# Turning the gathered rows while they are gathered, and a shorter routing stage, in a one-core hybrid layer with a mixture of experts

## What is computed

```
logits = x2 @ router_w + router_b                     # 32 experts
top_vals, top_idx = lax.top_k(logits, TOP_K)          # TOP_K = 4
gates = jax.nn.softmax(top_vals, axis=-1)
...
gu = xb @ w_gu[e] + b_gu[e]                           # rows of expert e, 1024 -> 2048
gate = jnp.minimum(gu[:, :D_FF], SWIGLU_LIMIT)
up = jnp.clip(gu[:, D_FF:], -SWIGLU_LIMIT, SWIGLU_LIMIT)
h = (up + 1.0) * (gate * jax.nn.sigmoid(SWIGLU_ALPHA * gate))
return h @ w_down[e] + b_down[e]                      # 1024 -> 1024
...
y = segment_sum(y_rows * row_w[:, None], row_tok)     # back to the tokens, weighted
```

## Time and profile before

| | |
|---|---|
| time, median of 3 runs | 1216.87 us (1216.04 to 1221.18) |
| the profiled execution's own time | 1217.71 us |
| its span, first to last instruction | 1215.9 us |
| TensorE busy | 1156.7 us, 95% |
| VectorE busy | 513.6 us, 42% |
| ScalarE busy | 254.9 us, 21% |
| bytes moved by DMA | 443.69 MB, mean 365 GB/s; 427 to 428 GB/s through the experts |
| first half and routing | 0 to 289.9 us |
| experts | 289.9 to 1198 us |
| last layer norm and output | 1198 to 1215.9 us |

### The profile page before, as it was taken

One profiled execution on the slowest core, in us unless ns is written; L12 is line 12 of the kernel. 1 busy time (PEld: TensorE's weight loads), 2 busy tenths in 40 slices (PEclk: granted clock), 3 DMA queues, 4 the chain that ended last, 5 costly groups with the idle time before them and its releaser, 6 DMA issues.

```text
span 1215.9 us, 14046 instructions
## 1 busy us (share of the span) xinstructions
PE 1156.7 (95%) x5736; PEld 562.1 (46%) x5736; DVE 513.6 (42%) x977; ACT 254.9 (21%) x398; POOL 3.2 (0%) x12
## 2 busy tenths in 40 slices
PE   9999999999999999999999998999999999999994
PEld 8989999654333333333333323333333333333331
DVE  4888878663333232223332222323222222222236
ACT  4645565311111111111111111111111111111112
POOL 1000000000000000000000000000000000000000
PEclk9999999999999999999999999999999999999998
DMA  9756754646999999999999999999999999999993
GB/s 234 237 168 206 230 146 143 263 179 258 408 430 428 425 429 428 428 426 426 430 427 425 429 427 427 429 427 426 428 428 427 427 428 428 426 427 429 427 424 154
DMA packets 93399, 443.69 MB, mean 365 GB/s; under 512 B 7848, under 2 KB 65336, under 8 KB 67998
## 3 DMA queue, kind: packets, MB, share of 16 engines
q1 hardware_dynamic: 93246, 442.67, 89.8%
q10 hardware_dynamic: 96, 0.22, 0.0%
HBM read 441.34 MB, written 1.53 MB: 364 GB/s over the span
## 4 chain that ended last, share of the span: by engine, by line
PE 57%; DMA 29%; DVE 10%; issue 2%; ACT 2%; DVEq 0%; SPq 0%; ACTq 0%
DMA ring<-in_w_gu 24%; PE PS L821 20%; PE PS L854 13%; PE PS L734 6%; PE PS L649 5%; DMA ring<-in_w_down 3%; PE PS L756 3%; PE PS L667 2%; DVE w_lo L960 2%; DVE tiles L998 2%; DVE tiles L1062 1%; PE PS L742 1%; PE PS L790 1%; PE PS L749 1%; PE PS L894 1%
## 5 line engine op out<-in xcount | busy, mean ns | idle before, releaser
L821 PE MATMUL PS<-ring,mid 128*64 128x512 f32 x1920 | 424.6, 596 | 24.5 <-DMA ring<-in_w_gu 24.5
L821 PEld LDWEIGHTS PS<-ring,mid 128*64 128x64 f32 x1920 | 135.6, 137 | 307.4 <-issue 256.2
L854 PE MATMUL PS<-ring,mid 128*64 128x512 f32 x960 | 212.6, 595 | 0.0
L1261 DVE TENSOR_SCALAR PS<-PS 128x512 f32<-128x512 f32 x30 | 21.0, 700 | 368.5 <-PE PS L821 368.5
L649 PE MATMUL PS<-x_hi,w_hi 128*128 128x320 f32 x448 | 142.4, 318 | 3.9 <-DVE w_lo L960 3.9
L649 PE MATMUL PS<-x_hi,w_lo 128*128 128x320 f32 x448 | 139.7, 312 | 0.0
L649 PE MATMUL PS<-x_lo,w_hi 128*128 128x320 f32 x448 | 139.7, 312 | 0.0
L1243 DVE TENSOR_TENSOR ys<-PS,ys 64x512 fp32r<-64x512 f32 x64 | 44.1, 689 | 200.7 <-ACT ys L567 190.8
L854 PEld LDWEIGHTS PS<-ring,mid 128*64 128x64 f32 x960 | 66.3, 137 | 130.8 <-issue 130.8
L998 DVE SCALAR_TENSOR_TENSOR x_tok<-PS,gate,x_tok 128x1024 f32<-128x1024 f32 (+1 forms) x93 | 115.1, 1276 | 19.7 <-PE PS L756 19.7
L558 ACT ACTIVATE mid<-PS 128x512 f32<-128x512 f32 x30 | 17.9, 597 | 434.2 <-DVE PS L1261 434.2
(11 more groups left out here) (225 smaller groups left out, 731.1 us busy)
## 6 DMA issues: line engine op xcount, KB each, us to landing
ring<-in_w_gu SPq DMA_DIRECT2D x124, 2048.0 KB, 40.0
ring<-in_w_down SPq DMA_DIRECT2D x62, 2048.0 KB, 38.9
raw<-in_w_in SPq DMA_DIRECT2D x56, 512.0 KB, 5.1
ring<-in_w_gu SPq DMA_DIRECT2D x8, 1024.0 KB, 7.4
ring<-in_w_out SPq DMA_DIRECT2D x4, 1024.0 KB, 6.1
ring<-in_w_down SPq DMA_DIRECT2D x4, 1024.0 KB, 41.6
x_tok<-in_x_prompt SPq DMA_DIRECT2D x1, 1024.0 KB, 6.2
out<-x SPq DMA_DIRECT2D x2, 512.0 KB, 2.7
```

What stands on the lines that cost most here:

```text
L821: last = mm(PS[64 * a:64 * a + 64, b, :], xgT[:, 2 * (u % 2) + j, u // 2, :], w[:, o:o + HALF], start=False, stop=(u == 3 and j == 1))
L854: last = mm(PS[64 * a:64 * a + 64, XB, :], hT[:, j, u, :], w[:, j * D + a * HALF:j * D + (a + 1) * HALF], start=(u == 0 and j == 0), stop= ...
L1261: dve.tensor_scalar(gm, gm, LIMIT, None, ALU.min).then_inc(gm_ok, 1)
```

## The change

Five things are done together.

1. `gather` now takes 128 columns of `x1` (every second one) as weights and lets the 64 columns of the one-hot table move, so that the gathered rows come out transposed. It has 8 blocks of 3 multiplications (the three tiles), 24 in all. `turn_x`, one of the two copies and the tile `xg_sb` are gone.
2. In the router the bias is added by TensorE, the logits are taken over tile by tile as they are ready, and the four best of each token are found with `match_replace` and a comparison instead of indices and one-hot sums. The gates come from an exponential over all 32 logits, masked.
3. `mask` and copies of `upper` and `ones` are of type fp32r, and the ranks take 3 multiplications instead of 9 (and 3 more for the counts behind them). `keep_warm` (one fp32r multiplication of 512 columns) replaces `keep_busy` in this stage.
4. The transposes of the position and gate tables (`turn_tables`) move behind the second unit of the first expert, and that expert's `gated_bias` between and into its down units.
5. For the last expert the sums of the one before stand one half unit later (`half == 1`).

The core of the diff:

```
             def gather(count):
                 pe.wait_ge(oh_ok, count)
-                for t, (t0, n) in enumerate(TILES):
-                    for a in range(2):
-                        last = mm(PS[64 * a:64 * a + 64, XB, :], onehot[0:n, t, :],
-                                  x1[0:n, t, a * HALF:(a + 1) * HALF], start=(t == 0), stop=(t == 2))
-                last.then_inc(xg_done, 1)
-
-            def turn_x(src, done):
-
                 for v in range(2):
                     for j in range(2):
-                        last = pe.transpose(PS[:, TB, (2 * v + j) * P:(2 * v + j + 1) * P],
-                                            src[:, 2 * P * v + j:2 * P * (v + 1):2], ident[:, :])
-                last.then_inc(done, 1)
+                        for a in range(2):
+                            first, o = a * HALF + 2 * P * v + j, ((2 * v + j) * 2 + a) * ROWS
+                            for t, (t0, n) in enumerate(TILES):
+                                last = mm(PS[:, XB, o:o + ROWS], x1[0:n, t, first:first + 2 * P - 1:2],
+                                          onehot[0:n, t, :], start=(t == 0), stop=(t == 2))
+                last.then_inc(xg_done, 1)
...
                 if i + 1 < NE:
                     if i + 1 not in ALONE:
                         add_bias(1 - s)
-                    pe.wait_ge(xg_ok, 2 * it + (rows_in(i) + 1))
-                    pe.wait_ge(hT_ok, 2 * it + (i + 1))
-                    turn_x(xg_sb, tx_done)
+                    pe.wait_ge(xgT_ok, 2 * it + (rows_in(i) + 1))
...
+            for q, t in enumerate(T_ORDER):
+                n = TILES[t][1]
+                dve.wait_ge(lg_done, q + 1)
+                link(dve.tensor_copy(lg[0:n, t, 0:NE], PS[0:n, LG_BANK[t], t * NE:(t + 1) * NE]))
+                link(dve.max(top[:, t, :], lg[:, t, 0:NE]))
+                dve.tensor_scalar(ek[:, t, :], lg[:, t, 0:NE], top[:, t, 0:1], None, ALU.subtract).then_inc(top_ok, 1)
+                link(dve.memset(top[:, t, TOPK:], LOWEST))
+                link(dve.match_replace(left[:, t, :], top[:, t, :], lg[:, t, :], HIGHEST))
+                last = dve.tensor_tensor(mask[:, t, :], left[:, t, 0:NE], lg[:, t, 0:NE], ALU.is_gt)
...
+            mm(PS[:, 5, 0:3 * NE], upper_r[:, :], mask[:, :, :].rearrange("p t e -> p (t e)"), start=True, stop=False)
+            mm(PS[:, 5, NE:3 * NE], ones_r[:, :], mask[:, 0:2, :].rearrange("p t e -> p (t e)"),
+               start=False, stop=False)
+            mm(PS[:, 5, 2 * NE:3 * NE], ones_r[:, :], mask[:, 0, :], start=False, stop=True).then_inc(rank_done, 1)
...
-                    if u == 0 and half == 0:
+                    if u == 0 and half == 1:
```

More of the change, by code:

```diff
@@ L197, in hybrid_layer @@
         mid = place("mid", [P, MID_SIZE // 4], MID)
-        xg_sb, xgT_f = (mid[:, i * HALF:(i + 1) * HALF] for i in range(2))
+        th_last, xgT_f = (mid[:, i * HALF:(i + 1) * HALF] for i in range(2))
         ys = place("ys", [P, 2, HALF], MID + 8 * HALF, F32R)
@@ L611, in _, with keep_warm @@
             mm = pe.matmul
+            def keep_warm(n, bank):
+                for _ in range(n):
+                    mm(PS[:, bank, :], ones_r[:, :], bias4[:, 0, :], start=True, stop=True)
             def keep_busy(n, bank):
@@ L697, in logits @@
                 t0, n = TILES[t]
+                out = PS[0:n, LG_BANK[t], t * NE:(t + 2) * NE]
+                mm(out, ones[0:1, 0:n], rb[0:1, :], start=True, stop=False)
+                if q == 2:
+                    keep_warm(3, 1)
                 pe.wait_ge(x1T_ok, q + 1)
                 for k in range(KC):
-                    last = mm(PS[0:n, 4, t * NE:(t + 1) * NE], xT[:, k, t0:t0 + n], rw[:, k, :],
-                              start=(k == 0), stop=(k == KC - 1))
+                    blocks = min(2, KC - k)
+                    last = mm(out[:, 0:blocks * NE], xT[:, k, t0:t0 + n],
+                              rw[:, k:k + blocks, :].rearrange("p a e -> p (a e)"), start=False, stop=(k == KC - 1))
                 return last
             pe.wait_ge(misc_in, 32)
+            pe.wait_ge(pad_ok, 1)
+            pe.wait_ge(consts_r, 1)
+            pe.wait_ge(bias_ok, 1)
             turn_x1(0)
@@ L711, in _ @@
             last.then_inc(so_turned, 1)
-            logits(0)
-            logits(1)
-            keep_busy(3, 1)
+            logits(0).then_inc(lg_done, 1)
+            logits(1).then_inc(lg_done, 1)
+            keep_warm(1, 1)
             turn_x1(2)
-            keep_busy(2, 1)
             logits(2).then_inc(lg_done, 1)
-            keep_busy(12, 1)
+            keep_warm(5, 1)
             pe.wait_ge(mask_ok, 1)
[L721 to L726, removed]
+            mm(PS[:, 5, 0:3 * NE], upper_r[:, :], mask[:, :, :].rearrange("p t e -> p (t e)"), start=True, stop=False)
+            mm(PS[:, 5, NE:3 * NE], ones_r[:, :], mask[:, 0:2, :].rearrange("p t e -> p (t e)"),
+               start=False, stop=False)
+            mm(PS[:, 5, 2 * NE:3 * NE], ones_r[:, :], mask[:, 0, :], start=False, stop=True).then_inc(rank_done, 1)
+            for t in range(3):
+                last = mm(PS[:, 4, 3 * NE:4 * NE], ones_r[:, :], mask[:, t, :], start=(t == 0), stop=(t == 2))
+            last.then_inc(cnt_done, 1)
+            keep_warm(3, 1)
             pe.wait_ge(so_ok, 1)
@@ L961, in split_low @@
                                   ALU.subtract).then_inc(lo_ok, 1)
+            dve.wait_ge(const_ok, 3)
+            dve.tensor_copy(upper_r[:, :], upper[:, :])
+            dve.tensor_copy(ones_r[:, :], ones[:, :]).then_inc(consts_r, 1)
             split_low(0)
@@ L1144, in _ @@
-            link(dve.tensor_copy(small[:, 0:1], ones[:, 0:1]))
-            link(dve.tensor_tensor(lg[0:NS, 2, :], PS[0:NS, 4, 2 * NE:3 * NE], rb[0:NS, :], ALU.add))
-            for t in range(3):
-                last = dve.max(top[:, t, :], lg[:, t, :])
-            link(last)
-            for t in range(3):
-                last = dve.max_index(idx[:, t, :], top[:, t, :], lg[:, t, :])
-            link(last)
-            dve.tensor_copy(idf, idx)
-            dve.tensor_tensor(ek, top[:, :, 0:TOPK], top[:, :, 0:1].to_broadcast([P, 3, TOPK]), ALU.subtract)\
-               .then_inc(top_ok, 1)
@@ L1155, in _ @@
-            dve.wait_ge(top_ok, 1)
-            for t in range(3):
-                last = dve.tensor_tensor(oh4[:, t], iota[:, 0:NE].unsqueeze(1).to_broadcast([P, TOPK, NE]),
-                                         idf[:, t, 0:TOPK].unsqueeze(2).to_broadcast([P, TOPK, NE]), ALU.is_equal)
-            link(last)
-            link(dve.tensor_reduce(mask, oh4.rearrange("p t k e -> p t e k"), AX_X, ALU.add))
-            dve.memset(mask[NS:P, 2, :], 0.0).then_inc(mask_ok, 1)
-            dve.wait_ge(exp_ok, 1)
@@ L1173, in _, with choose @@
+            last.then_inc(mask_ok, 1)
+            def choose(par, e):
+                return dve.tensor_copy(esel4[:, par], where4[:, :, ds(e, 1)].to_broadcast([P, 2, ROWS]))
+            choose(0, 0)
             dve.memset(pos4, 0.0)
+            dve.wait_ge(mask_ok, 1)
             dve.wait_ge(rank_done, 1)
-            dve.tensor_copy(cnt, PS[:, 5, 3 * NE:4 * NE])
-            link(stt(posm[:, :, :], PS[:, 5, 0:3 * NE].rearrange("p (t e) -> p t e", t=3), 1.0, mask, ALU.add, ALU.mult))
-            link(dve.tensor_scalar(posm[:, :, :], posm[:, :, :], -1.0, None, ALU.add))
+            link(stt(posm[:, :, :], PS[:, 5, 0:3 * NE].rearrange("p (t e) -> p t e", t=3), 1.0, mask_f, ALU.add, ALU.mult))
```

163 lines of the change are left out of this document (83 added, 80 removed).

## The result

| | before | after |
|---|---|---|
| time, median | 1216.86 us | 1426.27 us (1424.22 to 1429.02, 4 runs) |
| ratio | | 1.1715, 95% interval 1.1684 to 1.1746 |
| span of the profiled execution | 1215.9 us | 1422.5 us |
| granted clock, mean | 0.992 | 0.902 |
| DMA, mean | 365 GB/s | 312 GB/s |

The change costs 209 us. The forecast was 1390 us with a range up to 1415; the time lies 11 us beyond its top. First the windows of the changed kernel (columns as in the earlier trace rows), then lines of its page: the slices of the granted clock, the chain that ended last, and the group of the new gather.

A forecast was written before the change was run, and what follows sets the result against it. TensorE was to replace DMA as the bound, at 30.9 us an expert. Start 287.5, 30 x 30.95, single places and the end sum to 1309 us; clock falls of +54 to +108 give 1390, range 1246 to 1415.

The forecast's parts named there:

- the threshold: In the experts' stage, any TensorE period above 28.4 us an expert is paid, 30 times.
- the cover: The lead of 10 weight units (49 us of transfers) already there when expert 0 starts, used up over the experts.
- The gather's size: The new gather in each expert takes 8 blocks of 0.92 us, 7.3 us, row changes included.
- The bound of 5.5 for free changes: If row changes cost nothing, the gather takes 5.5 us and the kernel 1251 us; chance 0.14.
- The clock falls in each gather: TensorE drops to 1.2 GHz in each gather: 1363 to 1417 us, taken as 1390; chance 0.50.
- one slow stretch of 1.75 us (1363) and two (1417): Dense work slowed by 1.75 us once for each of 31 gathers, +54 us, or twice, +108 us.
- The reason for the fall: Row changes empty TensorE's array 16 times in the gather's 7.3 us, so the clock level falls.
- The stretch that the prediction held against a fall, 268 to 272 us: Before the experts, only 32-column multiplications and transposes, without row changes or gaps; the clock stayed at 1.00.
- the rival built on that mechanism, 1309 us: The gather never idles, so the clock stays high; TensorE bound at 30.9 us an expert, 1309 us; chance 0.28.
- The routing: Ahead of expert 0, `posm` at 278.3, gather at 279.2 for 284.1, first unit at 287.5, 2.4 us earlier.
- Expert 16: Its gather can't hide: 11.6 us between units where 8.8 were, plus 1.75 us of low clock behind it.
- the other cases: Clock stays high, 1309 us (0.28); row changes free, 1251 (0.14); gather at most 4.5 us, 1212 (0.08).

The follow-up runs named there:

- Number 4: The changed kernel with the 64-row token tile padded by zeros to 128 rows, 48 instructions without row changes: 1257.69 us.
- number 5: The changed kernel with the gather's two 128-row tiles first for all 8 blocks, then the 64-row tile, two row changes for 16: 1302.82 us.
- number 3: The changed kernel with the table moving twice (128 columns for 64) in 7 of 8 gather blocks, same loads and row changes: 1359.13 us.
- number 9: Number 4 with its first three gather blocks issued a second time, 66 instructions without row changes: 1332.96 us.
- numbers 5 to 7: number 5, number 6, and the changed kernel with two gather blocks behind each of an expert's four gate/up units (1415.80 us).
- number 1: The changed kernel with the old gather, `turn_x` and the two copies put back: 1213.02 us.
- number 6: The changed kernel with each gather from the second on cut in three, 3, 3 and 2 blocks behind the last three gate/up units: 1404.49 us.

## Why the prediction was right or wrong

**What bounds, and the threshold: right.** TensorE became the bound with the ring full, no wait on `ring` is left, SyncE waits for `used`, and DMA's share is 0.85 to 0.87. Number 4 bears out how close the cover ran: from its first unit (288.38) to the end of expert 29 (1185.14) are 896.8 us, 30 periods of 29.3 and what expert 16 costs more (two starts of L831 there are 43.9 us apart). That is 44 more than the 852.8 of before. The first unit starts 1.5 us earlier and the end is 2.1 us shorter (71.1 for 73.2), which leaves 40; the spans differ by 40.3 (1256.2 - 1215.9).

**The gather's size: a little small, and the first term that was mis-sized.** A block was put at 0.57 + 3 x 0.115 = 0.92 us and takes 0.99, so 7.9 us for 7.3 at the upper clock. Changes of rows do cost time, as forecast: from start to start 48 instructions take 5.56 us with none and 8 x 0.99 = 7.9 with 16, so 2.3 us or 0.15 us each, where the sum had 1.8 us; the two changes of number 5 cost 0.13 us each (645.45 - 639.63 = 5.82 us). The bound of 5.5 for free changes is near too. The Trainium skill (TensorE: Matmul & The Clock Gate, section on LDWEIGHTS) gives 107 ns for a load of 128 columns whatever its rows; by that, an estimate, the gather would be 5.1 us. Here a load on full rows takes 116 ns (629.66 - 621.98 = 7.68 us for 66), and between changing rows 165 ns (7.9 / 48): near the rule in the first case, not in the second.

**The clock falls in each gather: right, but what it costs came out by luck.** The prediction took the middle between one slow stretch of 1.75 us (1363) and two (1417), which is 2.6 us a gather. Neither case happened. The earlier trace rows show single low stretches and can't say whether a second follows; it does in nearly every expert, 6.8 us in all, but the two together cost less than 3.5 us. At the upper clock the period would be 27.02 - 3.34 + 7.92 = 31.6 us; it is 34.13, so they cost 2.5. In 6.8 us at the low level the gather and the small sums get done what takes 4.3 at the upper one; I had priced each stretch by a dense unit. The number of stretches was too small and the price of one too high, and the middle hides both.

**Which step failed.** The forecast's sum is 34 us short of the profiled execution (1390 for 1424.2), and the clock's term isn't where it is lost. 17 us are the period: 30.95 + 2.6 = 33.6 us forecast, 34.13 measured, 30 times, which is the gather's 0.92 us for a block of 0.99. The other 17 us are single places, priced nearly as if the clock were up in them: 8.4 at expert 16, 2.7 at the first unit (290.18 for 287.5), 7.0 at experts 0 to 2 and at the entry of the loop (the starts of L831 of experts 0 to 3 are 36.2, 35.7 and 35.5 us apart); the end takes 0.8 less than forecast. The figure of 1417 for two stretches is near the result because its clock term, some 30 us too high, makes up for most of these.

**The reason for the fall: wrong as stated.** "The array is emptied 16 times in 7.3 us" would hold for number 3 as well, with the same loads and changes, and there the clock stays up. No row shows the array being emptied either; what rows show is the time that a change costs. The stretch that the prediction held against a fall, 268 to 272 us, is a weaker counterexample than it says: its multiplications of 32 columns load only 64 columns of weights each (the form 128*64 in the row below). What is shown: with the same loads, moving twice the columns keeps it up (number 3); with 64 columns, full rows keep it up, even for 7.87 us (number 9). With 64 columns and a 64-row load in every third product, in one stretch, it falls every time. So in this kernel it takes both, the few moving columns and the 64-row loads with their changes; either remedy is enough. The changes alone are not the reason, and neither is the length alone. No run parts the half-filled loads from the changes; number 5, where the clock falls in most experts with two changes left of 16, says that many changes aren't needed. What decides in between, where the same instructions now meet a fall and now don't (numbers 5 to 7), is not settled by these runs.

```profile
268.68 3.02 PE L700 MATMUL PS<-rw,xT 128*64 128x32 f32 x32
```

The Trainium skill (same page, section on HAM oscillation) ties the fall to stretches in which TensorE idles. The changed kernel has no idle time ahead of the falls in 340 to 640 us, where TensorE is busy 300.00 of 300.00 us, so that rule alone doesn't explain it; the rival built on that mechanism, 1309 us, fails with it.

**The routing: the work right, the gain lost to the clock.** The rows of the changed kernel:

```profile
276.21 0.26 DVE L1008 SCALAR_TENSOR_TENSOR posm<-PS,mask 128x96 f32<-128x96 f32 x1
```

```profile
277.24 11.01 PE L744 MATMUL PS<-onehot,x 128*128 128x64 f32 x48
288.18 1.22 PE L791 MATMUL PS<-bias,esel 128*128 128x512 f32 x2
...
290.18 9.09 PE L826 MATMUL PS<-ring,mid 128*64 128x512 f32 x32
```

`posm` comes 2.1 us before the forecast of 278.3, since VectorE starts on the last logits at 274.29 instead of 276.45. That is no gain of the routing: the whole first half ended 2.3 us earlier in this execution (its last transposes begin at 263.82, before at 266.15). From there to the gather are 13.4 us, before 17.9, so 4.5 are saved; 4.9 were forecast. But the first gather takes 11.0 us, not 7.3, and the first unit starts at 290.18, not at 287.5: no better than before. With the old gather put back (number 1), the gather starts at 279.08 and the first unit at 284.33, 5.5 us before. Of these 0.5 us are an earlier first half (its last transposes begin at 265.66). The routing's gain is real, and it reaches the end of that kernel (5.8 us).

**Expert 16: too small.** It issues its gather itself, behind a wait, with the clock low through nearly all of it (0.65 in 850 to 852 us, then 0.50 up to 870):

```profile
840.91 7.09 PE L864 MATMUL PS<-ring,mid 128*64 128x512 f32 x32
850.86 13.35 PE L744 MATMUL PS<-onehot,x 128*128 128x64 f32 x48 [2.86 <-DVE esel L1167]
...
866.05 16.44 PE L826 MATMUL PS<-ring,mid 128*64 128x512 f32 x64
```

From the end of the down units (840.91 + 6.92) to the next unit are 18.2 us, where I had 11.6 and, with two slow stretches, 15.1; the units behind take 16.4 for 15.65. With 1.0 us more in the gather and the small work of expert 15 (its gather takes 10.86 us for 9.55), that is the 8.4 us above: two starts of L831 are 882.42 - 826.53 = 55.9 us apart, 21.8 over the period, where the sum had 11.6 + 1.75 = 13.35.

**What was wrong in the range.** I gave this mechanism 0.50, and set the range's top at 1415, short of my own figure of 1417 for its plainest form, with no room for a gather that is a little longer or for single places that run at the low level. The lower ends of the other cases held most of the room.

## What to carry to other kernels

Where few columns move, price a matrix product on TensorE by its weight loads, not by its arithmetic: here 12 instructions with 512 moving columns and a 4-piece turn (3.4 us) were replaced by 48 with 64 moving columns, which take 5.75 us at the best measured here. Where many loads follow each other with few columns moving, try keeping the weights' rows equal (pad the short tile with zeros: 1426 to 1258 us here), or letting more columns move (1359 us); read the granted clock in short windows behind such a place before costing it at the upper level. And take a change apart: its other parts, with the old gather kept, give 1213.02 us, a ratio of 0.9955 (0.9939 to 0.9971) to before, the only version here that is faster than the kernel before.

## What the runs showed that I had not expected

- More work made the kernel faster, twice: 128 moving columns in place of 64 (1359 us), and 66 instructions without changes of rows in place of 48 with them (1333 us), against 1426.
- Where the clock falls, the period settles on nearly one value in three kernels: 34.13 us in the changed kernel, 34.16 with three parts and 34.13 to 34.20 with four, though at the upper clock the first would take 31.6 and the second takes 32.50. (Number 5, with a shorter gather, settles on 30.8.) Cutting the gather moved the place of the fall and not the period. I have no shown cause for that.
- The executions of number 6 differ more than those of the others with the same instructions: 13 us among three of them (1392.89 to 1405.72), and a fourth at 1420.76 with a lower mean clock, while others stay within 6. In the profiled one some experts have a low clock and others don't.
